# Squared norms of q and k: summed by products with a column of ones instead of a split and a row of ones

## The chip, the cores and the metric
One core of one Trainium2 chip. The metric is the device time of one execution in microseconds, the median of several runs. The engines are TensorE (PE: matmuls, with PEld for its weight loads), VectorE (DVE), ScalarE (ACT), GpSimd (POOL) and SyncE (SP), which mostly issues transfers.

## The reference
One step of a decoder layer with two groups of heads, for one prompt of 1024 tokens behind 16 meta tokens and for 8 running sequences of 4 tokens. All is float32. Of the inputs of the gated delta rule, q and k are normed by head:

```python
def l2norm(x):
    return x * lax.rsqrt(jnp.sum(x * x, axis=-1, keepdims=True) + EPS)
...
xn = rmsnorm(h, norm_mix)
z = xn @ w_in
qkv, new_qkv = causal_dwconv(z[..., O_QKV:O_G], buf_qkv, conv_qkv_w)
qkv = jax.nn.silu(qkv.astype(f32))
q = l2norm(qkv[..., :nq].reshape(bsz, t, GDN_HEADS, GDN_DK)) * (GDN_DK ** -0.5)
k = l2norm(qkv[..., nq:2 * nq].reshape(bsz, t, GDN_HEADS, GDN_DK))
```

There are 4 heads of 128 features for q and for k. Behind them stand the chunked delta rule, a norm with a gate, the output projection and a feed-forward part of 4096 hidden units.

## The kernel before
**Layout.** All 1072 tokens (32 of the samples, 16 meta, 1024 of the prompt) lie along the free axis, features along the partitions: `kf` and `qf` are 128 x 4 x 1072, a slice per head. Tokens come in nine tiles: tile 0 has the first 48 (`C0`), tiles 1 to 8 have 128 each. `GROUPS` are three runs of columns for matmuls: 304, 384 and 384 wide.

**Input projection.** `IN_TILES` lists 28 output tiles of 128 features: 4 of k, 4 of q, 4 of v, 4 of the gate, then 12 for the short convolution. Tile n and group g make unit u = 3n + g. Each unit is 24 dense matmuls (`dense_part`, L1341 to L1343: weights and activations are split in a high and a low fp32r part, three products for each of 8 slices). A loop over the 84 units is written out for each engine, and small work is hung on fixed units by hand. ScalarE takes k, q and v out of the banks, VectorE runs the causal convolution (`conv_tap`), ScalarE applies silu, and then makes the squares. GpSimd makes the low part of each weight tile (`w_low`), and SyncE's load of a later weight tile waits for that.

**The squared norms.** They have to be summed over the partitions and must stand with the tokens along the partitions in the end, as `dst[:, tile, head]`. For head j (0 to 3 are k, 4 to 7 are q): `square(j)` on ScalarE writes the float32 square and a copy rounded to fp32r; `square_low(j)` on VectorE (unit 6 + 3j) subtracts one from the other; `sum_squares(j)` on TensorE (unit 7 + 3j) moves the high and the low part through `pick`, a matrix of zeros with one column of ones that is placed so that each head and group has a row of its own among 12. After four heads `keep_rows` copies the 12 rows out of bank 7, `turn_squares` (units 17 and 29) turns them by nine transposes, and `keep_norms` adds EPS. ScalarE then takes roots, and `scale_norms_k` and `scale_norms_q` make the factors.

**Around it.** From unit 18 on, for each tile: `decay_rows` (L1463), `decay_diff` (L2109), the exp on ScalarE, from unit 19 on `products_kk` (L1476) and `keep_at` (L2117), and spills to DRAM by SyncE. `small_solve` (units 28, 29) and `solve` (units 30 to 38; L2137, L2139) on VectorE invert the triangular blocks by substitution; SyncE writes the result to `X_kept` and `Y_kept`. Tile 0's own steps stand at units 30 to 50: `sample_products` (L1600, units 36 and 37), `use_state0`, `next_state0` (L1625, L1626, unit 41), whose o goes through VectorE and ScalarE's squares (L1170). Then ScalarE loads At, X and Y for tile 1 (L1115 and on), and `level_p` (L1514) opens the first round at unit 42. `keep_last` (L1949) copies the last rows of the convolution, which `turn_last` (L1406) has turned.

Of the kernel before, what the change touches and what calls it, by code (L numbers as in the profile page):

```python
# [7 lines left out]
ALU = mybir.AluOpType  # L8
# [5 lines left out]
P = 128  # L14
# [79 lines left out]
def build(nc, x_prompt, x_sample, state_conv_a, state_conv_qkv, state_ssm, meta_tokens, norm_mix, w_in,  # L94
# [4 lines left out]
    with ctx:  # L99
# [14 lines left out]
        def place(name, shape, dt, offset):  # L114
            return nc.alloc_sbuf_tensor_at(name, shape, dt, offset=offset)
# [46 lines left out]
        abT = place("abT", [16, TOK], F32, RK + 4 * SLOT)  # L162

        sq = [place(f"squares{i}", [P, TOK], F32, RYA + i * SLOT) for i in range(2)]
        sq_h = [place(f"squares_high{i}", [P, TOK], F32R, RYA + (2 + i) * SLOT) for i in range(2)]
        sq_l = [place(f"squares_low{i}", [P, TOK], F32R, RYA + (4 + i) * SLOT) for i in range(2)]
        NROW = 3 * NH
        pick = place("pick", [P, 2 * NROW], F32R, RYA + 6 * SLOT)
        ssr = place("ss_rows", [NROW, 3 * P], F32, RYA + 7 * SLOT)

        cm = small("c_main", [P, 2 * P + 2 * C0 + 2 * NH])
        eye, upper = cm[:, 0:P], cm[:, P:2 * P]
# [128 lines left out]
        last_sent = [sem("last_sent0"), sem("last_sent1")]  # L301
        ya_high_s = sem("ya_high_s")
        ya_low_s = sem("ya_low_s")
        sq_full = sem("sq_full"); sq_high = sem("sq_high"); sq_low = sem("sq_low"); pick_set = sem("pick_set")
        ss_rows = sem("ss_rows"); ss_turned = sem("ss_turned"); ss_done = sem("ss_done")
        norms_mid = sem("norms_mid"); norms_root = sem("norms_root"); norms_done = sem("norms_done")
        s_levels = sem("s_levels"); s_ahead = sem("s_ahead"); s_states = sem("s_states")

# [449 lines left out]
        def _(pool):  # L758
# [98 lines left out]
                sh = SSs[h // 2][:, h % 2, :, :]  # L857
                pool.tensor_tensor(sh, sh, eg_seq[:, :, h:h + 1].to_broadcast([P, NSEQ, P]), ALU.mult).then_inc(ss_decayed, 1)

            def pick_column():  # L860
                pool.memset(pick[:, :].bitcast(F32), 0.0).then_inc(pick_set, 1)
                pool.wait_ge(pick_set, 1)
                pool.memset(pick[:, NROW:NROW + 1].bitcast(F32), 1.0).then_inc(pick_set, 1)

            for n in range(N_IN):
                kind, i, _ = IN_TILES[n]
                if kind in ("k", "q", "v"):
                    history(n)
                if n == 0:
                    pool.wait_ge(x_low, 3 * KT)  # L870
                    pick_column()
                if n == 1:
                    zero_pairs()
                if n == 2:
                    identities()
                if kind == "H":
                    history_a(i)
                if n + 1 < N_MIX:
                    split_low(n + 1)
                for u in range(3 * n, 3 * n + 3):  # L880
                    t, s = round_step(u)
                    if u == TILE0["k"]:
                        beside()
                    if u == TILE0["sample"][-1]:
                        decay_states(0)
                        decay_states(1)
                    if u == TILE0["use"]:
                        decay_states(2)
                        decay_states(3)
                    if u == TILE0["states"]:  # L890
                        power(0)
                    if s == 3 and t >= 2:
                        power(t - 1)
                    if u % 3 == 2 and has_last(n):
                        last_columns(n)
# [69 lines left out]
        def _(act):  # L965
# [67 lines left out]
            def square(j):  # L1033

                src = (kf if j < NH else qf)[:, j % NH, :]
                act.wait_ge(silu_done, j + 1)
                if j >= 2:
                    act.wait_ge(sq_low, j - 1)
                act.activation(sq[j % 2][:, :], src, ACT.Square).then_inc(sq_full, 1)
                act.wait_ge(sq_full, j + 1)  # L1040
                if j >= 2:
                    act.wait_ge(ss_done, j - 1)
                act.activation(sq_h[j % 2][:, :], sq[j % 2][:, :], ACT.Copy).then_inc(sq_high, 1)

            def norm_roots(i):
                n = sc[("nk", "rq_s")[i]]
# [287 lines left out]
        def _(pe):  # L1334
# [92 lines left out]
            def sum_squares(j):  # L1427

                if j == 0:
                    pe.wait_ge(pick_set, 2)  # L1430
                if j == NH:
                    pe.wait_ge(norms_mid, 1)
                pe.wait_ge(sq_low, j + 1)
                i = j % NH
                for m, g in enumerate((1, 0, 2)):
                    c0, w = GROUPS[g]
                    row = NH * g + i
                    for part in (sq_h, sq_l):
                        ins = pe.matmul(ps[7][0:NROW, 0:w], pick[:, NROW - row:2 * NROW - row], part[j % 2][:, c0:c0 + w],
                                        start=(i == 0 and m == 0 and part is sq_h),  # L1440
                                        stop=(i == NH - 1 and m == 2 and part is sq_l))
                ins.then_inc(ss_done, 1)

            def turn_squares(i):
                pe.wait_ge(ss_rows, i + 1)
                for t in range(NT):
                    o, c = tile_cols(t)
                    g = [t in x for x in GTILES].index(True)
                    o -= GROUPS[g][0]
                    ins = pe.transpose(ps[7][0:c, NROW * t:NROW * t + NROW], ssr[:, o:o + c], eye[0:NROW, 0:NROW])  # L1450
                ins.then_inc(ss_turned, 1)


            def decay_rows(t):

# [240 lines left out]
            for n in range(N_IN):  # L1696
                kind, i, _ = IN_TILES[n]
                for g in range(3):
                    u = 3 * n + g
                    if n:  # L1700
                        if g == 0:
                            pe.wait_ge(w_low, n + 1)
                        if u == 3:
                            pe.wait_ge(rows_kept, 3)
                        if u >= 4:
                            acc_free(pe, (u - 4) // 3, (u - 4) % 3)
                        dense_part(n, g, normed, range(KT))
                    if u == 5:
                        turn_ab()
                    if u == 8:  # L1710
                        sum_g()
                    if u % 3 == 1 and 7 <= u < 7 + 6 * NH:
                        sum_squares((u - 7) // 3)
                    if u in (17, 29):
                        turn_squares(0 if u == 17 else 1)
                    if ROWS_AT <= u < ROWS_AT + NT:
                        decay_rows(u - ROWS_AT)
                    if KK_AT <= u < KK_AT + NT:
                        products_kk(u - KK_AT)
                    if g == 2 and 1 <= n <= LAST_LAST:  # L1720
                        turn_last(n - 1, L_BANK)
                    tile0_step(u)
                    t, s = round_step(u)
                    if s:
                        round_part(t, s)
                    if u in TURN_H:
                        pe.wait_ge(vn_kept, min(t, NT))
                        turn_last(TURN_H[u], M_BANK)
# [156 lines left out]
        def _(dve):  # L1885
# [105 lines left out]

            nk, rk, c_, p_ = sc["nk"], sc["rk"], sc["c"], sc["p"]

            def square_low(j):
                dve.wait_ge(sq_high, j + 1)
                if j >= 2:
                    dve.wait_ge(ss_done, j - 1)
                dve.tensor_tensor(sq_l[j % 2][:, :], sq[j % 2][:, :], sq_h[j % 2][:, :].bitcast(F32),
                                  ALU.subtract).then_inc(sq_low, 1)

            def keep_rows(i):
                dve.wait_ge(ss_done, NH * (i + 1))
                dve.wait_ge(ss_turned, i)
                dve.tensor_copy(ssr[:, :], ps[7][0:NROW, 0:3 * P]).then_inc(ss_rows, 1)

            def keep_norms(i):

                dst = (nk, sc["rq_s"])[i]
                dve.wait_ge(ss_turned, i + 1)
                link(dve.memset(dst[:, 0, :], 1.0))  # L2010
                for g, ts in enumerate(GTILES):
                    turned = ps[7][:, 0:NROW * NT].rearrange("p (t r) -> p t r", r=NROW)
                    r0 = NH * g
                    if g == 0:
                        dve.tensor_scalar(dst[0:C0, 0, :], turned[0:C0, 0, r0:r0 + NH], EPS, None, ALU.add)
                        ts = ts[1:]
                    ins = dve.tensor_scalar(dst[:, ts[0]:ts[-1] + 1, :], turned[:, ts[0]:ts[-1] + 1, r0:r0 + NH],
                                            EPS, None, ALU.add)
                ins.then_inc(norms_mid, 1)

            def scale_norms_k():

# [331 lines left out]
            for n in range(N_IN):  # L2354
                kind, i, _ = IN_TILES[n]
                for g in range(3):
# [10 lines left out]
                        ab_second()  # L2367
                    if u == 9:
                        g_keep()
                    if u % 3 == 0 and 6 <= u < 6 + 6 * NH:  # L2370
                        square_low((u - 6) // 3)
                    if u in (16, 28):
                        keep_rows(0 if u == 16 else 1)
                    if u in (17, 29):
                        keep_norms(0 if u == 17 else 1)
                    if ROWS_AT <= u < ROWS_AT + NT:
# [194 lines left out]
```

## Time and profile before

| | us |
|---|---|
| median of 3 runs | 1363.97 (1362.43 to 1364.47) |
| the profiled execution's own time | 1363.06 |
| its span, first to last instruction | 1361.2 |
| TensorE matmul busy in it | 1329.1 |
| VectorE, ScalarE, GpSimd busy | 826.5, 413.6, 536.5 |

The rows below come from the profiled execution; its own time is 1.9 us above its span. A busy TensorE is not TensorE at its peak: matmuls are pipelined, so the time that one costs is the distance of its start from the next start, not the duration in its record. A product of plain float32 leaves two records, a transpose or an fp32r matmul one.

### The profile page before, as it was taken

The numbers are of one execution on the slowest core, as the hardware profiler recorded it, in microseconds if no ns is written. First come the engines' busy times: TensorE is split into PE (matmuls) and PEld (weight loads), VectorE is DVE, ScalarE is ACT, GpSimd is POOL, SyncE is SP. The second block draws the span as 40 slices with busy tenths as digits, with TensorE's granted clock in tenths as the row PEclk, the third lists the DMA queues.
The fourth block names the chain that finished last, engine by engine and source line by source line (L and its number), as shares of the span: only waits on it lengthen the run. The fifth ranks groups of instructions, "written<-read, shape, count | busy, mean of one in ns | idle before, by whom it ended". The sixth has DMA issues, their size and how long they took to land.

```text
span 1361.2 us, 22593 instructions
## 1 busy us (share of the span) xinstructions
PE 1329.1 (98%) x9089; PEld 1297.2 (95%) x9089; DVE 826.5 (61%) x1376; ACT 413.6 (30%) x812; POOL 536.5 (39%) x550
## 2 busy tenths in 40 slices
PE   6999999899999999999999999999999999999997
PEld 4899999799999999999999999999999999999997
DVE  4466689533644536555675666756666567566855
ACT  6566552111222212332032222222222223222312
POOL 2232123211112111211257557475674665746811
PEclk9999998999999999999999999999999999999999
DMA  6123553643332222321211212112012121111212
GB/s 189 38 67 101 145 156 101 153 135 83 83 88 63 78 71 75 91 80 37 57 31 47 63 32 63 47 47 63 32 47 63 32 64 37 57 47 34 77 43 117
DMA packets 161850, 99.88 MB, mean 73 GB/s; under 512 B 19639, under 2 KB 156371, under 8 KB 161746
## 3 DMA queue, kind: packets, MB, share of 16 engines
q1 hardware_dynamic: 137216, 85.31, 21.6%
q10 hardware_dynamic: 24530, 13.13, 3.6%
q8 instruction: 72, 1.18, 0.4%
q14 instruction: 32, 0.26, 0.1%
HBM read 77.62 MB, written 20.80 MB: 72 GB/s over the span
## 4 chain that ended last, share of the span: by engine, by line
PE 85%; DVE 7%; DMA 3%; ACT 2%; issue 1%; POOL 1%; SPq 1%; DVEq 0%; ACTq 0%; POOLq 0%
PE banks L1817 9%; PE banks L1819 9%; PE banks L1818 9%; PE banks L1341 8%; PE banks L1343 8%; PE banks L1342 8%; PE banks L1836 7%; PE banks L1837 7%; PE banks L1835 7%; DVE inverse L2139 2%; DVE outer L2137 2%; PE banks L1851 1%; PE banks L1514 1%; PE banks L1852 1%; PE banks L1853 1%
## 5 line engine op out<-in xcount | busy, mean ns | idle before, releaser
L1817 PE MATMUL banks<-hg_high,w_high 128*128 128x384 f32 (+1 forms) x768 | 249.5, 325 | 0.5 <-POOL w_low L906 0.5
L1819 PE MATMUL banks<-hg_high,w_low 128*128 128x384 f32 (+1 forms) x768 | 247.6, 322 | 0.0
L1818 PE MATMUL banks<-hg_low,w_high 128*128 128x384 f32 (+1 forms) x768 | 247.3, 322 | 0.0
L2474 DVE TENSOR_TENSOR hT<-hT,banks 128x528 f32<-128x528 f32 x280 | 189.5, 701 | 84.4 <-PE banks L1837 75.4
L1341 PE MATMUL banks<-xn_high,w_high 128*128 128x384 f32 (+1 forms) x672 | 228.0, 339 | 0.1
L1343 PE MATMUL banks<-xn_high,w_low 128*128 128x384 f32 (+1 forms) x672 | 219.8, 327 | 0.0
L1342 PE MATMUL banks<-xn_low,w_high 128*128 128x384 f32 (+1 forms) x672 | 219.8, 327 | 0.0
L774 POOL TENSOR_TENSOR w_low<-w_raw,w_high 128x1024 fp32r<-128x1024 f32 x37 | 90.5, 2447 | 265.4 <-ACT w_high L982 265.4
L1817 PEld LDWEIGHTS banks<-hg_high,w_high 128*128 128x128 f32 x768 | 144.2, 188 | 2.5 <-POOL w_low L906 2.3
L1818 PEld LDWEIGHTS banks<-hg_low,w_high 128*128 128x128 f32 x768 | 144.3, 188 | 0.1
L1819 PEld LDWEIGHTS banks<-hg_high,w_low 128*128 128x128 f32 x768 | 144.2, 188 | 0.0
L925 POOL TENSOR_TENSOR w_low<-w_pair,w_high 128x256 fp32r<-128x256 f32 x140 | 104.0, 761 | 67.0 <-ACT w_high L1296 67.0
L1341 PEld LDWEIGHTS banks<-xn_high,w_high 128*128 128x128 f32 x672 | 128.1, 191 | 2.0 <-DVE xn_low L1915 0.6
L906 POOL TENSOR_TENSOR w_low<-w_raw,w_high 128x1024 fp32r<-128x1024 f32 x31 | 78.7, 2537 | 126.8 <-ACT w_high L1278 126.8
L1342 PEld LDWEIGHTS banks<-xn_low,w_high 128*128 128x128 f32 x672 | 128.3, 191 | 0.0
L2453 DVE TENSOR_TENSOR u_row<-banks,h_squares 128x384 f32<-128x384 f32 (+1 forms) x96 | 50.1, 522 | 128.3 <-PE banks L1819 128.1
L1343 PEld LDWEIGHTS banks<-xn_high,w_low 128*128 128x128 f32 x672 | 127.7, 190 | 0.0
L1837 PE MATMUL banks<-op_high_T,w_low 128*128 128x264 f32 x448 | 127.7, 285 | 0.0
L1836 PE MATMUL banks<-op_low_T,w_high 128*128 128x264 f32 x448 | 127.7, 285 | 0.0
L1835 PE MATMUL banks<-op_high_T,w_high 128*128 128x264 f32 x448 | 127.1, 284 | 0.0
L1296 ACT ACTIVATE w_high<-w_pair 128x256 fp32r<-128x256 f32 x140 | 55.4, 415 | 177.9 <-PE banks L1819 84.6
L1837 PE MATMUL banks<-op_high_B,w_low 128*128 128x264 f32 x336 | 95.8, 285 | 0.0
(316 smaller groups left out, 2804.5 us busy)
## 6 DMA issues: line engine op xcount, KB each, us to landing
w_raw<-in_w_up SPq DMA_DIRECT2D x32, 512.0 KB, 4.1
w_pair<-in_w_down SPq DMA_DIRECT2D x32, 512.0 KB, 3.4
w_raw<-in_w_in SPq DMA_DIRECT2D x28, 512.0 KB, 4.4
w_raw<-in_w_out SPq DMA_DIRECT2D x8, 512.0 KB, 4.1
x_slice<-in_x_prompt SPq DMA_DIRECT2D x8, 512.0 KB, 4.1
out<-y_tok SPq DMA_DIRECT2D x8, 512.0 KB, 2.6
x_tok<-in_x_prompt SPq DMA_DIRECT2D x2, 1536.0 KB, 15.8
v_kept_rows<-v_feat SPq DMA_DIRECT2D x4, 536.0 KB, 3.2
```

The costliest lines, as they stand in the source:

```text
L774: pool.tensor_tensor(w_l[n % 2][:, :, :], w_raw[n % 2][:, :, :], w_h[n % 2][:, :, :].bitcast(F32), ALU.subtract).then_inc(w_low, 1)
L925: pool.tensor_tensor(set_of(w_l, b, s), set_source(n, PRODUCTS[x][0]), set_of(w_h, b, s).bitcast(F32), ALU.subtract).then_inc(w_low, 1)
L1341: pe.matmul(bank[:, 0:w], w_h[n % 2][:, k, :], hi[:, c0:c0 + w], start=(k == first), stop=False)
L1342: pe.matmul(bank[:, 0:w], w_h[n % 2][:, k, :], lo[:, c0:c0 + w], start=False, stop=False)
L1343: ins = pe.matmul(bank[:, 0:w], w_l[n % 2][:, k, :], hi[:, c0:c0 + w], start=False, stop=(k == last))
L1817: pe.matmul(bank[:, 0:w], w_h[half][:, k, :], hg_h[:, k, c0:c0 + w], start=(k == 0), stop=False)
L1818: pe.matmul(bank[:, 0:w], w_h[half][:, k, :], hg_l[:, k, c0:c0 + w], start=False, stop=False)
L1819: ins = pe.matmul(bank[:, 0:w], w_l[half][:, k, :], hg_h[:, k, c0:c0 + w], start=False, stop=(k == KT - 1))
L1835: pe.matmul(bank, high[:, j, :], op_h[name][:, j, cols], start=(j == 0), stop=False)
L1836: pe.matmul(bank, high[:, j, :], op_l[name][:, j, cols], start=False, stop=False)
L1837: ins = pe.matmul(bank, low[:, j, :], op_h[name][:, j, cols], start=False, stop=(j == FB // 2 - 1))
L2474: dve.tensor_tensor(hc, hc, both, ALU.add if sign > 0 else ALU.subtract).then_inc(acc_read_dve, 1)
```

## The change
The split and the turning fall away. `square(j)` makes only the float32 square. `sum_squares(j)` takes the square of each token tile as the stationary operand (128 x 128, or 128 x 48 for tile 0) and moves one column of ones, so that the sums come out with the tokens along the partitions, in column 8t + j of bank 7: nine plain float32 products for a head. `keep_norms` reads them from there.

```diff
-        sq_h = [place(f"squares_high{i}", [P, TOK], F32R, RYA + (2 + i) * SLOT) for i in range(2)]
-        sq_l = [place(f"squares_low{i}", [P, TOK], F32R, RYA + (4 + i) * SLOT) for i in range(2)]
-        NROW = 3 * NH
-        pick = place("pick", [P, 2 * NROW], F32R, RYA + 6 * SLOT)
-        ssr = place("ss_rows", [NROW, 3 * P], F32, RYA + 7 * SLOT)
...
-            def pick_column():
-                pool.memset(pick[:, :].bitcast(F32), 0.0).then_inc(pick_set, 1)
-                pool.wait_ge(pick_set, 1)
-                pool.memset(pick[:, NROW:NROW + 1].bitcast(F32), 1.0).then_inc(pick_set, 1)
...
                 if j >= 2:
-                    act.wait_ge(sq_low, j - 1)
+                    act.wait_ge(ss_done, j - 1)
                 act.activation(sq[j % 2][:, :], src, ACT.Square).then_inc(sq_full, 1)
-                act.wait_ge(sq_full, j + 1)
-                if j >= 2:
-                    act.wait_ge(ss_done, j - 1)
-                act.activation(sq_h[j % 2][:, :], sq[j % 2][:, :], ACT.Copy).then_inc(sq_high, 1)
...
             def sum_squares(j):
                 if j == 0:
-                    pe.wait_ge(pick_set, 2)
+                    pe.wait_ge(ab_kept, 2)
                 if j == NH:
                     pe.wait_ge(norms_mid, 1)
-                pe.wait_ge(sq_low, j + 1)
-                i = j % NH
-                for m, g in enumerate((1, 0, 2)):
-                    c0, w = GROUPS[g]
-                    row = NH * g + i
-                    for part in (sq_h, sq_l):
-                        ins = pe.matmul(ps[7][0:NROW, 0:w], pick[:, NROW - row:2 * NROW - row], part[j % 2][:, c0:c0 + w],
-                                        start=(i == 0 and m == 0 and part is sq_h),
-                                        stop=(i == NH - 1 and m == 2 and part is sq_l))
-                ins.then_inc(ss_done, 1)
-
-            def turn_squares(i):
-                pe.wait_ge(ss_rows, i + 1)
+                pe.wait_ge(sq_full, j + 1)
                 for t in range(NT):
                     o, c = tile_cols(t)
-                    g = [t in x for x in GTILES].index(True)
-                    o -= GROUPS[g][0]
-                    ins = pe.transpose(ps[7][0:c, NROW * t:NROW * t + NROW], ssr[:, o:o + c], eye[0:NROW, 0:NROW])
-                ins.then_inc(ss_turned, 1)
+                    ins = pe.matmul(ps[7][0:c, 2 * NH * t + j:2 * NH * t + j + 1], sq[j % 2][:, o:o + c], one[:, 0:1],
+                                    start=True, stop=True)
+                ins.then_inc(ss_done, 1)
...
-            def square_low(j):
-                dve.wait_ge(sq_high, j + 1)
-                if j >= 2:
-                    dve.wait_ge(ss_done, j - 1)
-                dve.tensor_tensor(sq_l[j % 2][:, :], sq[j % 2][:, :], sq_h[j % 2][:, :].bitcast(F32),
-                                  ALU.subtract).then_inc(sq_low, 1)
-
-            def keep_rows(i):
-                dve.wait_ge(ss_done, NH * (i + 1))
-                dve.wait_ge(ss_turned, i)
-                dve.tensor_copy(ssr[:, :], ps[7][0:NROW, 0:3 * P]).then_inc(ss_rows, 1)
...
             def keep_norms(i):
                 dst = (nk, sc["rq_s"])[i]
-                dve.wait_ge(ss_turned, i + 1)
+                sums = ps[7][:, 0:2 * NH * NT].rearrange("p (t j) -> p t j", j=2 * NH)[:, :, NH * i:NH * i + NH]
+                dve.wait_ge(ss_done, NH * (i + 1))
                 link(dve.memset(dst[:, 0, :], 1.0))
...
+                dve.tensor_scalar(dst[0:C0, 0, :], sums[0:C0, 0, :], EPS, None, ALU.add)
+                dve.tensor_scalar(dst[:, 1:NT, :], sums[:, 1:NT, :], EPS, None, ALU.add).then_inc(norms_mid, 1)
```

## Rows read from the trace of the kernel before

**Rows 1.** The page, busy us, share of the span and instructions.

```profile
PE 1329.1 (98%) x9089; PEld 1297.2 (95%) x9089; DVE 826.5 (61%) x1376; ACT 413.6 (30%) x812; POOL 536.5 (39%) x550
```

**Rows 2.** TensorE's waits: us in total, times, longest.

```profile
PE banks L1514 <- issue: 3.9, 1, 3.9
...
PE banks L1463 <- DVE decay L2109: 1.1, 1, 1.1
...
PE banks L1406 <- DVE last_out L1949: 0.5, 1, 0.5
```

**Rows 3.** Timelines of SyncE and ScalarE (start, us), DMA issues (KB, us to landing).

```profile
249.70 3.38 SPq L693 DMA_DIRECT2D Y_kept<-blocks  x1
...
Y_kept<-blocks SPq DMA_DIRECT2D x1, 512.0 KB, 8.2
...
256.44 0.19 ACT L1170 ACTIVATION_READ_ACCUMULATOR qs_scaled<-o_tok,rq_s 48x1 f32 x1
258.00 0.39 ACTq L1115 DMA_DIRECT2D At<-At_kept  x1
```

**Rows 4.** Timeline of VectorE, 177 to 248 us.

```profile
177.78 1.27 DVE L1998 TENSOR_TENSOR squares_low<-squares,squares_high 128x1072 fp32r<-128x1072 f32 x1 [2.66 <-ACT squares_high L1043]
178.97 1.12 DVE L2117 SCALAR_TENSOR_TENSOR At_spilled<-banks,p,decay 128x128 f32<-128x128 f32 x4
...
183.99 0.54 DVE L2004 COPY ss_rows<-banks 12x384 f32<-12x384 f32 x1
...
246.75 1.10 DVE L2142 COPY blocks<-inverse 128x1024 f32<-128x1024 f32 x1
```

**Rows 5.** Timeline of TensorE, one block of squares and one turning.

```profile
110.87 0.33 PE L1439 MATMUL banks<-squares_high,pick 128*12 128x384 f32 x1
...
111.84 0.33 PE L1341 MATMUL banks<-xn_high,w_high 128*128 128x384 f32 x1
...
115.85 0.34 PE L1343 MATMUL banks<-xn_high,w_low 128*128 128x384 f32 x1
116.12 0.69 PE L1450 MATMUL banks<-c_main,ss_rows 12*48 12x12 f32 x9
116.73 0.29 PE L1406 MATMUL banks<-c_main,last_in 128*27 128x128 f32 x1
```

**Rows 6.** Timeline of TensorE, the second half of the sample products.

```profile
227.15 3.64 PE L1600 MATMUL banks<-wq_sample,S_sample 128*128 128x8 f32 x32
230.64 0.42 PE L1341 MATMUL banks<-xn_high,w_high 128*128 128x384 f32 x1
230.90 0.34 PE L1342 MATMUL banks<-xn_low,w_high 128*128 128x384 f32 x1
```

**Rows 7.** Timeline of TensorE, `turn_ab`.

```profile
61.24 0.34 PE L1343 MATMUL banks<-xn_high,w_low 128*128 128x384 f32 x1
61.51 2.13 PE L1412 MATMUL banks<-c_main,abT 16*48 16x8 f32 x18
63.57 0.29 PE L1406 MATMUL banks<-c_main,last_in 128*27 128x128 f32 x1
```

**Rows 8.** Timeline of TensorE, decay rows and kk products at unit 19.

```profile
126.04 1.05 PE L1463 MATMUL banks<-c_main,g 128*128 128x128 f32 x8
127.03 0.56 PE L1476 MATMUL banks<-k_feat 128*48 128x48 f32 x8
```

**Rows 9.** Timeline of TensorE, the last kk products (unit 27).

```profile
174.85 1.05 PE L1476 MATMUL banks<-k_feat 128*128 128x128 f32 x8
```

**Rows 10.** Stretches: us, busy us of each engine, granted clock, DMA.

```profile
61.42:63.62 2.20, 2.20 (x21) 2.07 (x20) 0.00 (x0) 1.98 (x3) 0.98 (x5) 1.00 0.19 39
...
216.00:219.00 3.00, 2.84 (x27) 2.87 (x26) 2.90 (x4) 1.32 (x3) 2.48 (x3) 1.00 0.41 169
219.00:225.50 6.50, 6.50 (x24) 6.50 (x24) 6.12 (x13) 0.00 (x0) 0.51 (x1) 0.50 0.01 3
...
227.00:231.00 4.00, 4.00 (x36) 4.00 (x35) 3.79 (x9) 1.59 (x2) 0.14 (x1) 1.00 0.59 174
```

More of the change, by code:

```diff
@@ L303, in build @@
         ya_low_s = sem("ya_low_s")
-        sq_full = sem("sq_full"); sq_high = sem("sq_high"); sq_low = sem("sq_low"); pick_set = sem("pick_set")
-        ss_rows = sem("ss_rows"); ss_turned = sem("ss_turned"); ss_done = sem("ss_done")
+        sq_full = sem("sq_full")
+        ss_done = sem("ss_done")
         norms_mid = sem("norms_mid"); norms_root = sem("norms_root"); norms_done = sem("norms_done")
@@ L870, in _ @@
                     pool.wait_ge(x_low, 3 * KT)
-                    pick_column()
                 if n == 1:
@@ L1713, in _ @@
                         sum_squares((u - 7) // 3)
-                    if u in (17, 29):
-                        turn_squares(0 if u == 17 else 1)
                     if ROWS_AT <= u < ROWS_AT + NT:
@@ L1992, in _ @@
             nk, rk, c_, p_ = sc["nk"], sc["rk"], sc["c"], sc["p"]
-            def square_low(j):
-                dve.wait_ge(sq_high, j + 1)
-                if j >= 2:
-                    dve.wait_ge(ss_done, j - 1)
-                dve.tensor_tensor(sq_l[j % 2][:, :], sq[j % 2][:, :], sq_h[j % 2][:, :].bitcast(F32),
-                                  ALU.subtract).then_inc(sq_low, 1)
-            def keep_rows(i):
-                dve.wait_ge(ss_done, NH * (i + 1))
-                dve.wait_ge(ss_turned, i)
-                dve.tensor_copy(ssr[:, :], ps[7][0:NROW, 0:3 * P]).then_inc(ss_rows, 1)
             def keep_norms(i):
                 dst = (nk, sc["rq_s"])[i]
-                dve.wait_ge(ss_turned, i + 1)
+                sums = ps[7][:, 0:2 * NH * NT].rearrange("p (t j) -> p t j", j=2 * NH)[:, :, NH * i:NH * i + NH]
+                dve.wait_ge(ss_done, NH * (i + 1))
                 link(dve.memset(dst[:, 0, :], 1.0))
[L2011 to L2019, printed above, removed]
+                dve.tensor_scalar(dst[0:C0, 0, :], sums[0:C0, 0, :], EPS, None, ALU.add)
+                dve.tensor_scalar(dst[:, 1:NT, :], sums[:, 1:NT, :], EPS, None, ALU.add).then_inc(norms_mid, 1)
             def scale_norms_k():
@@ L2369, in _ @@
                         g_keep()
[L2370 to L2373, printed above, removed]
                     if u in (17, 29):
```

## Prediction
> **What bounds the kernel now.** I read the page first: TensorE is busy for 1329.1 of 1361.2 us [rows 1], so a microsecond of work put on it or taken from it is a microsecond of the end, unless a wait lies behind it that swallows it. So the next view is the list of TensorE's waits. The changed code runs between 61 and 190 us. Behind the first changed block only three waits are worth the name until the first round starts: 1.1 us for `decay_diff`, 0.5 us for `keep_last`, and the large one, 3.9 us of matmul idle before `level_p` (L1514) at 263 us [rows 2]. Everything on VectorE and ScalarE is of interest only where it feeds one of these.
>
> The third view is the chain of work, of which I took the pieces in order of time, and the timelines of VectorE, ScalarE and SyncE before 263 us. `level_p` waits for At. Its load is issued by ScalarE at 258.00 us. ScalarE has two things to get through before it: the squares of tile 0's o, whose last piece is at 256.44 us (they follow VectorE's o and that follows TensorE's `next_state0`, unit 41), and the landing of Y_kept, issued at 249.70 us and landed 8.2 us later, at 257.9 us [rows 3]. Y_kept landed last, and ScalarE had been free since 256.6 us: 1.3 us of slack on the branch that hangs on TensorE. Y_kept comes from the substitution on VectorE, which from 178.97 us to the copy at 246.75 us runs without a gap [rows 4].
>
> **What is removed from TensorE.** Eight blocks of six matmuls. One block stands from 110.87 to 111.84 us, so 0.97 us [rows 5]; the other seven have the same shapes: 8 x 0.97 = 7.8 us. Then twice nine turns: the matmul before them has its start at 115.85 us and passes the engine on 0.17 us later (the pitch of its neighbours), `turn_last` follows at 116.73 us: 0.70 us [rows 5], of which I leave 0.05 us for the change of operand that `turn_last` would then pay itself. 2 x 0.65 = 1.3 us. Together 9.1 us.
>
> **What is added to TensorE.** 72 float32 products, nine in a block, with a stationary tile of 128 x 128 (128 x 48 for tile 0) and one moving column. The trace has no product with one column, but two near ones. The sample products (L1600) have a 128 x 128 float32 stationary tile and 8 moving columns: 16 of them (32 records, so two for each product) take from 227.15 to 230.64 us, and the dense matmul behind them has a pitch of 0.26 instead of 0.17 us: 3.58 us, 0.224 us for one [rows 6]. `turn_ab` is nine products over the same nine tiles with 8 columns: from 61.41 us (61.24 and 0.17) to 63.57 us, 2.16 us [rows 7]. A product costs its loads of 128 columns here, not its columns, so one column costs as 8 do. For a block I take 2.1 us, between 9 x 0.224 = 2.02 and 2.16. 8 x 2.1 = 16.8 us. Bounds: from above four products with 128 columns, 126.04 to 127.03 us, 0.248 us for one, 2.23 us for a block [rows 8]; from below the nine turns, which have one record each, 0.70 us for nine [rows 5].
>
> Here a rule speaks against the change. The trace shows two records for each float32 product and 0.224 us. The Trainium skill (FP8 and Floating Point Precision, on how floating point is handled) says that true FP32 takes four passes through the array, and its page TensorE: Matmul & The Clock Gate (LDWEIGHTS) that a load costs its columns at 1.2 GHz, 107 ns for 128. If every pass had its load, a product would cost 0.43 us as an estimate from these pages, a block 3.9 us; the trace has half of it.
>
> **The sum on TensorE.** 16.8 - 9.1 = +7.7 us (with 2.02 and 2.16: +7.1 and +8.2; with 2.23: +8.7).
>
> **What the other engines get rid of.** VectorE loses eight subtractions of 1.27 us and two copies of 0.54 us [rows 4], ScalarE one pass over 128 x 1072 for each head, which stands in the same chain, GpSimd two small fills. Up to 178 us these lie beside TensorE's dense matmuls; the relief is worth nothing by itself, but it shortens the chain by which `decay_diff` is late. Nothing new is late by the added waits: TensorE now waits for the square itself (ready two instructions earlier than the low part), ScalarE's square of head j waits for a block of TensorE that ran two heads before.
>
> **What the waits swallow.** From block to block TensorE falls behind its old times by 1.13 us (2.1 - 0.97), while the decay chain beside it gets shorter. By the last decay rows (unit 26) it is some 6 us later, so I let the 1.1 us wait go. For `keep_last` TensorE waits for VectorE's program, and that moves less, see below: 0.5 us goes too [rows 2]. TensorE thus reaches unit 41 later by 7.7 - 1.1 - 0.5 = 6.1 us. ScalarE's squares end at 256.63 + 6.1 = 262.7 us, the load of At goes out there and not at 258.00 us: +4.7 us.
>
> The other branch: `keep_at(8)` at 178.97 us stands behind the subtraction of 1.27 us and the wait for ScalarE's high part; its product on TensorE is at 174.85 us for 0.9 us [rows 4, 9]. With seven blocks and one turning (7 x 1.13 - 0.65 - 1.1 = +6.2 us) it is ready at 181.9 us, so VectorE starts its gapless stretch 3.0 us later than now, and loses 0.6 us inside it (the copy at 183.99 us, 0.54 us [rows 4], and two small additions). Y_kept lands 2.4 us later, at 260.3 us: before 262.7 us, so it is not what ends last any more. Behind `level_p` the order of work and its waits are as before, and 4.7 us stay.
>
> The profiled execution took 1363.06 us with a span of 1361.2 us; the median of the runs is 1363.97 us. The sum gives a span of 1361.2 + 4.7 = 1365.9 us, 1367.8 us for the profiled execution, which is 0.9 us below the median, and 1363.97 + 4.7 = **1368.7 us** as the median (+0.3%).
>
> **The clock.** TensorE's granted clock fell to its half (1.2 instead of 2.4 GHz) once near such work: the first half of the sample products ran from 216.2 us, and from 219 to 225.5 us the clock is 0.50; in the second half, same size, it stayed at 1.00, as in `turn_ab` [rows 10]. A dip costs half of 6.5 us, 3.3 us. The new blocks have 2.1 us each, the size of `turn_ab`. But those of units 19, 22 and 25 are followed at once by decay rows and kk products, over 1 us of short float32 products [rows 8], together nearly as long as the sample half that lost the clock.
>
> **Rivals.**
> 1. *The waits are not swallowed* (chance 0.17). They move with TensorE, because what they wait for is released by TensorE itself (`decay_diff` by the decay rows, At through unit 41). Against it: `decay_diff` sheds a pass of ScalarE and the 1.27 us of VectorE for each head, and Y_kept, which ends last now, doesn't hang on unit 41. Price: the whole 7.7 us, 1371.6 us.
> 2. *A dip of the clock in units 19 to 25* (0.09): 4.7 + 3.3 = 8.0 us, 1372.0 us; with two, 1375 us.
> 3. *The dip at 219 us doesn't come back* (0.12), because the sample products start at another time. TensorE is then only 2.8 us late at unit 41, Y_kept at 260.3 us ends last, +2.4 us: 1366.4 us, within what counts as no change.
> 4. *Faster* (0.04): a product with one column costs less than one with 8, because it needs no second record. At the price of a turn, 0.078 us, a block costs 0.70 us, TensorE gains 9.1 - 5.6 = 3.5 us, and VectorE, which idled 2.66 us ahead of the subtraction at 177.78 us for its operand [rows 4], can start its stretch up to 3.9 us earlier, so that both branches of At come 3.5 us earlier: 1360.5 us. It decides below 9.1 / 72 = 0.126 us for a product.
> 5. *Four loads a product* (0.03). A block would be twice 2.1 us, TensorE 33.6 - 9.1 = +24.5 us, less the same 3.0 us of waits and slack: 1385.5 us. This is the case that the pages of the Trainium skill named above would give; the two records of L1600 speak against it.
>
> **How the numbers follow.** The likeliest case (0.55) has its own range by the bounds of a block, 2.02 to 2.23 us, and by half of the swallowed microsecond more or less: 1367.4 to 1370.5 us. 8 in 10 take in rival 3 below, and rival 1 and the single dip above: 1366.1 to 1372.4 us. The measurement tells 0.2%, 2.7 us, from no change. Slower by more than that: likeliest, 1, 2 and 5, 0.84. Within it: rival 3 and the low end, 0.12. Faster: 0.04.
>
> **What would show it.** In the profile after: blocks of 18 records on the line of `sum_squares`, 2.0 to 2.2 us from the dense matmul before to the one behind; TensorE's busy time up by some 7 us; no wait at `decay_rows`; `keep_at(8)` some 3 us later; the load of At at 262.7 us, behind the o squares and not behind Y_kept, and `level_p` at 268.2 us. It is wrong if a block takes under 1.2 or over 3 us, if the clock row shows a dip before 190 us, or if Y_kept still ends last.

## The result, and the profile after
The changed kernel takes 1371.49 us in the median of six runs (1370.08 to 1375.9), the kernel before 1363.97 us. The two medians differ by 7.5 us (0.55%), where 4.7 us were forecast; the ratio on record is 1.0064 (interval 1.0048 to 1.0079). In two later series of runs the same program stood at 1.0086 (1.0065 to 1.0108) and 1.0102 (1.0086 to 1.0117). A series (the expectations below say "call") is made on one chip, with the kernel before in it.

TensorE's busy time went from 1329.1 us [rows 1] to 1342.6 us in the page after, in a profiled execution of 1372.73 us, 9.7 us above that of before:

```profile
PE 1342.6 (98%) x9167; PEld 1313.7 (96%) x9167; DVE 821.7 (60%) x1362; ACT 405.8 (30%) x804; POOL 538.4 (39%) x548
```

The timeline of TensorE has the block as expected: a clean one (head 2) with 18 records, from 102.67 us (102.50 and the pitch, the distance from one start to the next, of 0.17) to 104.76 us, and a pitch of 0.26 us in place of 0.17 behind it, so 2.18 us against 0.97 us [rows 5]. And it has something that was not expected of a block that stands alone between dense matmuls. Behind head 0 the same dense matmuls have a pitch of 0.32 us in place of 0.17:

```profile
70.42 2.12 PE L1421 MATMUL banks<-one,squares 128*48 128x1 f32 x18
72.41 0.65 PE L1326 MATMUL banks<-xn_high,w_high 128*128 128x384 f32 x1
72.86 0.52 PE L1327 MATMUL banks<-xn_low,w_high 128*128 128x384 f32 x1
73.18 0.52 PE L1328 MATMUL banks<-xn_high,w_low 128*128 128x384 f32 x1
73.50 0.52 PE L1326 MATMUL banks<-xn_high,w_high 128*128 128x384 f32 x1
...
102.50 0.34 PE L1328 MATMUL banks<-xn_high,w_low 128*128 128x384 f32 x1
102.77 2.12 PE L1421 MATMUL banks<-one,squares 128*48 128x1 f32 x18
104.76 0.42 PE L1326 MATMUL banks<-xn_high,w_high 128*128 128x384 f32 x1
105.02 0.34 PE L1327 MATMUL banks<-xn_low,w_high 128*128 128x384 f32 x1
```

The table of stretches after shows what goes with it. Its third value from the right is the granted clock: 3.4 us at half the clock (1.2 in place of 2.4 GHz) behind four of the eight blocks, those of heads 0, 1, 3 and 5. The first trace of before has no such stretch in this part:

```profile
72.50:75.90 3.40, 3.40 (x12) 3.40 (x12) 0.00 (x0) 0.00 (x0) 0.00 (x0) 0.51 0.52 157
89.60:93.00 3.40, 3.40 (x13) 3.40 (x12) 0.00 (x0) 0.60 (x5) 0.00 (x0) 0.51 0.90 259
120.30:123.70 3.40, 3.40 (x12) 3.40 (x11) 0.00 (x0) 0.00 (x0) 0.00 (x0) 0.51 0.31 94
154.20:157.60 3.40, 3.40 (x18) 3.40 (x18) 1.13 (x4) 0.44 (x1) 0.00 (x0) 0.52 1.15 347
```

I call such a stretch a dip. One loses 3.4 / 2 = 1.7 us of TensorE's work. Added up, the clock lost between 60 and 240 us is 10.2 us here (four dips of 3.4 us and one of 6.8 us, halved) and 3.4 us in the trace of before (the one dip of [rows 10], which came again at 229 us).

Of TensorE's waits, the two small ones are gone and the large one has shrunk from 3.9 to 2.4 us [rows 2]; L1485 is `level_p`:

```profile
PE banks L1485 <- DMA At<-At_kept: 2.4, 1, 2.4
```

Both branches of At came late together, and Y_kept, not the squares, still ended last: it is issued at 258.48 us and lands 8.2 us later, at 266.68 us, and the load of At goes out at 266.74 us; before it was 258.00 us [rows 3]. ScalarE's squares of o began at 265.96 us and ran on past the load, so the load does not wait for the last of them. `keep_at(8)` waits for TensorE's product and starts at 187.45 us, not 178.97 us [rows 4]. The timelines of VectorE, SyncE and ScalarE after:

```profile
187.45 1.13 DVE L2068 SCALAR_TENSOR_TENSOR At_spilled<-banks,p,decay 128x128 f32<-128x128 f32 x4 [1.38 <-PE banks L1447]
...
258.48 3.38 SPq L688 DMA_DIRECT2D Y_kept<-blocks  x1
...
266.74 0.39 ACTq L1100 DMA_DIRECT2D At<-At_kept  x1
266.75 0.39 ACT L1155 ACTIVATE qs_scaled<-o_tok,rq_s 48x128 f32<-48x128 f32 x1
```

From the first product of `turn_ab` (61.51 us before [rows 7], 60.62 us after; the start-up varies) to the first of `level_p` it is 202.0 us before and 212.4 us after. Behind `level_p` nothing is added: from there to the end it is 1361.2 - 263.5 = 1097.7 us before and 1370.6 - 273.05 = 1097.5 us after.

### The profile page after: what moved, and what is told of

It is laid out like the page before. It is cut to its first block, busy times and chain, and to the rows that moved or that the text cites. A ratio compares the mean times of both kernels' runs of the same rounds, so it can differ in the third digit from the quotient of the medians.

```text
span 1370.6 us, 22712 instructions
## 1 busy us (share of the span) xinstructions
PE 1342.6 (98%) x9167; PEld 1313.7 (96%) x9167; DVE 821.7 (60%) x1362; ACT 405.8 (30%) x804; POOL 538.4 (39%) x548
## 4 chain that ended last, share of the span: by engine, by line
PE 93%; DVE 3%; DMA 2%; ACT 1%; issue 1%; SPq 0%; DVEq 0%; ACTq 0%
PE banks L1326 10%; PE banks L1328 10%; PE banks L1327 10%; PE banks L1786 9%; PE banks L1788 9%; PE banks L1787 9%; PE banks L1805 7%; PE banks L1806 7%; PE banks L1804 7%; PE banks L1421 1%; PE banks L1820 1%; PE banks L1821 1%; PE banks L1822 1%; PE banks L1485 1%; PE banks L1499 1%; DMA x_tok<-in_x_prompt 1%
## 5 line engine op out<-in xcount | busy, mean ns | idle before, releaser
L1326 PE MATMUL banks<-xn_high,w_high 128*128 128x384 f32 (+1 forms) x672 | 231.0, 344 | 0.1
```

Of the source, the lines that this page charges most:

```text
L1326: pe.matmul(bank[:, 0:w], w_h[n % 2][:, k, :], hi[:, c0:c0 + w], start=(k == first), stop=False)
```

## The experiments
The theory formed on this: **time = work of the products as far as the waits don't hide it, plus 1.7 us for each dip, and a narrow block of 2.2 us is long enough for dips.** "Narrow" means few moving columns. The rival, **plain work**: the products and their changes of operand cost all of it, and the dips only stand beside them. A second rival: only a single moving column lets the clock fall. Each ratio is against the kernel before in the same series; runs 1 to 4 are one series, 5 to 8 the next, 9 to 11 the last.

**1. Blocks cut in two.** The same 72 products, five behind unit 7 + 3j and four behind unit 8 + 3j.

```diff
-                for t in range(NT):
+                for t in range(*PARTS[part]):
...
+            PARTS = [(0, 5), (5, 9)]
```

> The changed kernel, with each head's nine products cut into five behind unit 7 + 3j and four behind unit 8 + 3j; the products and their number stay. Clock theory (a block of 2.1 us without a wide moving operand halves TensorE's granted clock for 3.4 us in about half of the cases, four times 1.7 us in the profile): pieces of 1.2 us cause no or hardly any dips, the granted clock stays 1.00 before 200 us, and the time is 1365 to 1367 us, 5 to 6 us below the changed kernel's 1371.5. Rival, plain work (the products and their change of operand cost all of it, the dips only stand beside them): two entries in place of one cost a little more, 1371 to 1373 us.

1368.29 us (1367.39 to 1371.67), ratio 1.0052 (1.0038 to 1.0065). No dip between 60 and 220 us. The clock did what the theory says; the time, 6.0 us above before (1362.26 us in that series), is not the 1 to 3 us above it that the theory asked for. The changed kernel did not run in this series, and the interval of this ratio overlaps its first one (1.0048 to 1.0079), so runs 9 and 10 have to settle what the cut gains.

**2. One by one between the dense matmuls** of unit 8 + 3j.

```diff
+                    if between:
+                        between(k)
...
-                        dense_part(n, g, normed, range(KT))
+                        product = sum_squares((u - 8) // 3) if u % 3 == 2 and 8 <= u < 8 + 6 * NH else None
+                        dense_part(n, g, normed, range(KT), between=product)
```

> The changed kernel, with each head's products put one by one between the dense matmuls of unit 8 + 3j, one behind each slice of three and the ninth at the end. Clock theory: no dip before 200 us at all, and the time falls to that of the two-part kernel, 1365 to 1367 us, plus or minus what nine changes between operands cost: if a product beside dense matmuls costs 0.22 us as in the block, the same time; if its first load hides behind the dense matmul ahead of it, 0.1 us less for each of 72, down to 1360 us; if each change of operand costs the 0.09 us seen behind a block, 1371 us with a clock of 1.00. Plain work: 1371 us or more.

1369.71 us, ratio 1.0051 (1.0039 to 1.0063). The table of stretches has no dip from 70 to 220 us (the one before 70 us is behind `turn_ab`):

```profile
60.00:70.00 10.00, 10.00 (x62) 9.71 (x61) 7.36 (x12) 7.70 (x12) 4.49 (x9) 0.83 0.09 19
70.00:220.00 150.00, 150.00 (x1020) 146.60 (x1020) 93.73 (x223) 77.88 (x126) 33.10 (x48) 1.00 0.43 118
```

The timeline of TensorE shows what a product costs there:

```profile
75.81 0.34 PE L1328 MATMUL banks<-xn_high,w_low 128*128 128x384 f32 x1
75.98 0.28 PE L1424 MATMUL banks<-one,squares 128*128 128x1 f32 x2
76.12 0.42 PE L1326 MATMUL banks<-xn_high,w_high 128*128 128x384 f32 x1
76.38 0.34 PE L1327 MATMUL banks<-xn_low,w_high 128*128 128x384 f32 x1
```

Without the product, the two dense matmuls behind that of 75.81 us would start at 75.98 and 76.15 us; the second one starts at 76.38 us, so the product costs 0.23 us, about as in the block (2.18 / 9 = 0.24 us). Nothing of it hides behind the dense matmuls. The run is 7.4 us above before with no dip behind a product, so the work is the larger part of the loss.

**3. Seven moving columns** in place of one.

```diff
-                    ins = pe.matmul(ps[7][0:c, 2 * NH * t + j:2 * NH * t + j + 1], sq[j % 2][:, o:o + c], one[:, 0:1],
+                    at = 7 * (2 * NH * t + j)
+                    ins = pe.matmul(ps[7][0:c, at:at + 7], sq[j % 2][:, o:o + c], one[:, 0:1].to_broadcast([P, 7]),
                                     start=True, stop=True)
```

> The changed kernel, with seven moving columns of ones in place of one (each sum is written seven times). Clock theory in its general form (any narrow block counts): the dips stay, a block takes 2.1 to 2.2 us, 1371 to 1372 us. Rival: only the single column lets the clock fall (turn_ab, with 8 columns and the same length, has none): the dips vanish, 1365 to 1367 us. Plain work: no change, 1371.5 us, dips or not.

1368.66 us (1367.74 to 1375.72), ratio 1.006 (1.004 to 1.008). In its profile one dip behind a block and one behind `turn_ab`, which moves eight columns. So a single column is not needed for a dip, and the second rival falls. Whether seven make dips rarer, one profile can't tell: the median is below the 1371 to 1372 us expected with dips, two of the six executions took 1374.56 and 1375.72 us at a mean clock of 0.985, against 0.991 to 0.993 in the others, and the ratio is within the interval of the changed kernel.

**4. The passes of ScalarE and VectorE put back**, read by nobody.

```diff
+                act.activation(sq_h[j % 2][:, :], sq[j % 2][:, :], ACT.Copy).then_inc(sq_high, 1)
...
+                dve.tensor_tensor(sq_l[j % 2][:, :], sq[j % 2][:, :], sq_h[j % 2][:, :].bitcast(F32),
+                                  ALU.subtract).then_inc(sq_low, 1)
```

> The changed kernel, with ScalarE's eight copies to fp32r and VectorE's eight subtractions put back, though nobody reads them. Clock theory, with the passes beside TensorE's work: 1371 to 1373 us, the load of At at the same place. Rival (the relief of the two engines shortens a wait and hides some of the products' cost): slower by 1 to 4 us, 1373 to 1375 us, with waits of TensorE for the decay or for At back.

1374.04 us, ratio 1.0087 (1.0073 to 1.01), five dips from 60 to 200 us. That is the ratio of the changed kernel in the next series (1.0086) and below that of the last (1.0102), with a mean clock of 0.986 to 0.987 (0.983 to 0.990 there); no wait for the decay came back. The table under 6 shows the same: with its five dips taken off it reaches the sample products when the changed kernel does. The relief of the two engines is worth nothing that these runs can tell, but since the changed kernel did not run in this series, a microsecond or two of the whole time stays open.

**5. The kernel before, again.** 

> The kernel before, once more, beside the others on one chip, to have its marks and its dips from a second execution. Both theories: a ratio of 1.000 within 0.1%, no dip of the granted clock between 60 and 200 us, one or two in the sample products, one behind the wait for At; the first product of turn_ab between 59.5 and 61.5 us, since the start-up varies.

1363.76 us, ratio 1.0001 (0.9993 to 1.001). The expectation of no dip from 60 to 200 us missed: this execution has two there, one of them behind `turn_ab` (0.83 from 60 to 70 us in the table of stretches), the other behind a wait of 2.2 us for the decay:

```profile
60.00:70.00 10.00, 10.00 (x61) 9.96 (x61) 6.77 (x10) 9.12 (x15) 4.37 (x9) 0.83 0.04 9
...
170.00:176.00 6.00, 5.59 (x31) 5.49 (x32) 5.06 (x17) 4.00 (x6) 0.51 (x4) 0.72 0.50 148
```

`turn_ab`, the same block in the same program, has a dip in this execution and none in the first.

**6. The changed kernel, again.** 

> The changed kernel, once more, on the same chip. Clock theory: dips of 1.7 us each behind some of the eight blocks again, not behind the same ones, since they depend on where the block happens to fall; the executions differ by such steps; from turn_ab to the first sample product 159.9 us (two parts, no dip) plus 1.7 us for each dip; median 0.6 to 0.7% above before. Rival, plain work: the same distance with and without dips.

1374.0 us (1369.94 to 1380.18), ratio 1.0086. The results list a mean granted clock for each execution: 0.990 for 1369.94 us, 0.989 for 1373.53 and 1373.8, 0.987 for 1374.2, 0.984 for 1379.31, 0.983 for 1380.18. 0.007 of some 1370 us is 9.6 us, and the times differ by 10.2 us: as far as three decimals tell, the lost clock is paid in full. Its profile, of the fastest of them, has one dip behind `turn_ab` and three behind blocks, at 104, 172 and 193 us (heads 2, 6 and 7); in the first profile they were behind heads 0, 1, 3 and 5.

What the expectation set against plain work is the distance from the first product of `turn_ab` to the first of the sample products, read from the timeline of TensorE in each profile:

| profile | dips in between | distance, us |
|---|---|---|
| before; before, again | 0; 2 | 154.65; 157.90 |
| two parts (run 1; run 10) | 0; 1 | 159.95; 161.50 |
| between the dense matmuls (2) | 1 | 161.66 |
| seven columns (3) | 2 | 163.36 |
| changed kernel, first profile; again (6) | 4; 4 | 166.59; 166.53 |
| passes put back (4) | 5 | 168.05 |
| changed kernel, third time (9) | 6 | 169.62 |
| three parts (11) | 1, and a wait of 1.7 us | 163.21 |

From the two parts with no dip to the whole blocks with six it grows by 9.7 us, 1.6 us for each; the three parts come under 9 to 11. Without dips the change costs 159.95 - 154.65 = 5.3 us here, in two parts; with 1.6 us for each dip taken off, the whole blocks and the single products come to the same within 0.3 us. Plain work would have the same distance with and without dips, so this tells against it most directly.

**7. The kernel before without the low part** (the sums are those of squares rounded to fp32r).

```diff
-                act.activation(sq[j % 2][:, :], src, ACT.Square).then_inc(sq_full, 1)
-                act.wait_ge(sq_full, j + 1)
...
-                act.activation(sq_h[j % 2][:, :], sq[j % 2][:, :], ACT.Copy).then_inc(sq_high, 1)
+                act.activation(sq_h[j % 2][:, :], src, ACT.Square).then_inc(sq_high, 1)
...
-                    for part in (sq_h, sq_l):
```

> The kernel before without the low part: ScalarE writes the square rounded to fp32r, VectorE subtracts nothing, TensorE moves three runs of columns for a head instead of six; the sums are those of the rounded squares. TensorE loses 8 x 0.49 = 3.9 us of wide matmuls and no block is narrow. Clock theory: no dip, time 3 to 4 us below before as far as the wait for At lets it through, 1359 to 1362 us. Rival (Y_kept, not TensorE, sets the load of At, and it hangs on VectorE): VectorE's stretch starts earlier too, by the subtraction and its wait of 2.7 us, so the gain passes; if the stretch hung on the decay chain instead, no gain, 1362 to 1363 us.

1357.91 us (1357.18 to 1358.12), ratio 0.9958 (0.9945 to 0.997): 5.7 us faster, more than the 3.9 us of its matmuls. Y_kept goes out at 241.28 us and not at 249.70 us [rows 3]: VectorE's branch gained more than TensorE's (reckoned from `turn_ab`, `keep_at(8)` starts 8.0 us earlier and the first sample product 6.3 us), and At is loaded at 250.97 us. TensorE still waits 4.4 us there.

**8. The changed kernel with rounded squares** (the sums are those of squares rounded to fp32r): the square is written as fp32r, and two columns of ones in fp32r move.

```diff
-        sq = [place(f"squares{i}", [P, TOK], F32, RYA + i * SLOT) for i in range(2)]
+        sq = [place(f"squares{i}", [P, TOK], F32R, RYA + i * SLOT) for i in range(2)]
+        ones_r = place("ones_rounded", [P, 2], F32R, RYA + 6 * SLOT)
...
-                    ins = pe.matmul(ps[7][0:c, 2 * NH * t + j:2 * NH * t + j + 1], sq[j % 2][:, o:o + c], one[:, 0:1],
+                    ins = pe.matmul(ps[7][0:c, at:at + 2], sq[j % 2][:, o:o + c], ones_r[:, 0:2],
```

> The changed kernel with the square rounded to fp32r by ScalarE as the stationary operand and two columns of ones in fp32r moving; the sums are those of the rounded squares. It keeps the form of the block and halves its records: one load for each product, 0.08 to 0.11 us, a block of 0.8 to 1.1 us as in the turns of before. Clock theory: blocks so short cause no dip; TensorE has 8 x 1.0 = 8 us instead of 9.1 us: 1360 to 1363 us, at or 1 us below before. Plain work: the same by another road (half of 17.4 us is gone): 1362 to 1363 us; it is told apart from the clock theory by the clock alone, here.

1357.39 us (1355.26 to 1359.11), ratio 0.9956 (0.9943 to 0.9968). The timeline has one record for a product, a block of 70.93 - 70.01 = 0.92 us and 0.09 us of longer pitch behind it:

```profile
70.01 1.06 PE L1426 MATMUL banks<-ones_rounded,squares 128*48 128x2 f32 x9
70.93 0.42 PE L1328 MATMUL banks<-xn_high,w_high 128*128 128x384 f32 x1
71.19 0.34 PE L1329 MATMUL banks<-xn_low,w_high 128*128 128x384 f32 x1
```

The table of stretches has a clock of 1.00 up to 200 us:

```profile
60.00:200.00 140.00, 140.00 (x952) 138.04 (x951) 92.07 (x217) 83.04 (x131) 36.06 (x57) 1.00 0.43 119
```

It was forecast at 1360 to 1363 us: the work is as forecast, and the rest goes with VectorE's earlier start (`keep_at(8)` 5.1 us earlier, reckoned from `turn_ab`), as in 7. This version and 7 beat both kernels, with the sums rounded; the runs don't tell which of the two is faster.

**9 to 11. Whole blocks, two parts and three parts in one series.** The third kernel has three products behind each of the units 7, 8 and 9 + 3j (`PARTS = [(0, 3), (3, 6), (6, 9)]`).

> The changed kernel, a third time, so that the two cuts of its blocks stand beside it on one chip. Time theory now: before + 6 us for the work of the products, as far as waits don't hide it, + about 1.6 us for each dip beyond those of before; with three to five dips 1370 to 1374 us, and within its executions the slower ones have the lower mean clock (0.983 for 1380 us, 0.990 for 1370 us in the execution list of the second call). Rival: the mean clock doesn't order them.

> The blocks of nine cut into five and four, again. Time theory: 6 us above before, mean clock as before (0.992 to 0.994), so 2 to 5 us below the whole blocks in the same call. Rival, plain work: no difference from the whole blocks.

> The blocks of nine cut into three times three, behind units 7 + 3j, 8 + 3j and 9 + 3j. Time theory: the dips were already gone with two parts, so that a third entry only adds its change of operand, 8 x 0.1 to 0.2 us: 6 to 8 us above before, clock as before. Rival (the dips get rarer with every cut): below the two parts by 1 to 2 us.

| | median | ratio | clock lost, 60 to 218 us, in the profile |
|---|---|---|---|
| before, same series | 1362.67 | | |
| whole blocks | 1374.93 (1373.82 to 1379.4) | 1.0102 (1.0086 to 1.0117) | 10.2 us, six dips, one of them behind `turn_ab` |
| two parts | 1369.69 (1367.78 to 1374.09) | 1.0056 (1.0044 to 1.0069) | 1.7 us, one dip, behind `turn_ab` |
| three parts | 1372.97 (1371.88 to 1375.32) | 1.0076 (1.0064 to 1.0088) | none; one dip at 219.28 us |

The tables of stretches of the whole blocks and of the two parts:

```profile
90.00:100.00 10.00, 10.00 (x58) 9.93 (x58) 1.78 (x4) 4.91 (x10) 1.60 (x4) 0.83 0.43 107
...
145.00:165.00 20.00, 20.00 (x134) 19.74 (x133) 11.33 (x29) 10.28 (x15) 2.48 (x2) 0.91 0.50 140
165.00:185.00 20.00, 20.00 (x133) 19.74 (x132) 11.97 (x31) 9.58 (x14) 2.83 (x5) 0.91 0.51 143
185.00:205.00 20.00, 20.00 (x130) 19.66 (x129) 16.80 (x54) 10.63 (x16) 4.88 (x7) 0.91 0.39 104
```

```profile
60.00:70.00 10.00, 10.00 (x61) 9.71 (x61) 7.40 (x12) 7.75 (x12) 4.49 (x9) 0.83 0.11 26
70.00:200.00 130.00, 130.00 (x898) 127.03 (x897) 74.75 (x182) 69.42 (x111) 30.26 (x43) 1.00 0.38 104
```

One cut, with the same 72 products, takes 5.2 us off the median, and the dips behind blocks with it: plain work falls. In run 9 too the slower executions have the lower mean clock (0.989 for 1373.82 us, 0.984 for 1378.97 and 1379.4 us).

A second cut has no dips left to take and costs 3.3 us. The changes of operand are not the reason: at 203.99 us, at a product of `turn_last` behind the last block, the three parts are 143.3 us behind `turn_ab`, and the two parts of run 1 are 143.5 us behind it at the same product (203.30 us). What comes then stands in the profile of the three parts: `keep_norms` for q on VectorE waits 4.7 us for the last three products, in the stretch that ran without a gap before (0.8 us in the two parts), and TensorE waits 1.7 us for `keep_last`, where the two parts don't wait. Behind that wait stands a dip. The lines are of VectorE's timeline, TensorE's waits and the stretches:

```profile
194.77 0.06 DVE L1973 MEMSET rq_s<- 128x4 f32 x1 [4.72 <-PE banks L1423]
...
PE banks L1391 <- DVE last_out L1923: 1.7, 1, 1.7
...
218.00:224.00 6.00, 6.00 (x34) 5.95 (x35) 5.69 (x13) 3.06 (x5) 0.99 (x3) 0.72 0.59 184
```

The wait and the dip together make the 163.21 - 159.95 = 3.3 us by which the three parts reach the sample products later than the two parts of run 1. This is one profile, and no run put the last products back to test it.

## Why the prediction was off
**The step that failed is the one on the clock.** It says that the new blocks have the size of `turn_ab`, where the clock stayed at 1.00, sees a danger only in units 19, 22 and 25, where short products follow, and gives it a chance of 0.09; the sum itself has nothing for it. Three of the four dips of the first profile are behind blocks that stand between dense matmuls (heads 0, 1 and 3). Over the three profiles of the changed kernel it is 5 of 9 blocks in units 19, 22 and 25 and 7 of 15 of the others, so what follows a block made no difference that can be seen. `turn_ab` itself has a dip in 6 of the 13 profiles, among them that of the kernel before, again: one trace of one execution was read as a property of the block. The runs give for it 5.2 us between whole blocks and two parts in one series, and three to five dips of 1.7 us behind the blocks in each of the three profiles. Each was half of what the prediction priced, 3.3 us, which is the dip of 6.8 us in [rows 10].

**The work of the products** was right in kind and a little small: 2.18 us for a block, not 2.1 us, 8 x 0.08 = 0.6 us more. By the sample products the change without dips is 5.3 us late, in the profile of run 1, where 6.1 us were forecast. In whole times the two parts stand 6.0 and 7.0 us above before, against the 4.7 us forecast; some of their executions have dips too, as the profile of run 10 shows, and how the rest divides is open.

**The waits** for the decay and for `keep_last` went as forecast, and that at `level_p` shrank [rows 2]. So rival 1, whose 1371.6 us is nearly the measured time, is not what happened: the waits did swallow their part, and the dips put as much back. Its number was right by accident.

**At's two branches.** Without dips, VectorE's branch moved as worked out: in the first run of the two parts `keep_at(8)` starts 2.8 us later than before, reckoned from `turn_ab` (180.10 - 59.83 against 178.97 - 61.51 us), where 3.0 us were forecast. But the 0.6 us that the stretch was to lose did not show: it ran to 249.08 us, 1.2 us longer than before, 0.8 us of it a wait of `keep_norms` for the products of the second part. Y_kept took 9.2 us to land, not 8.2, and still ended last there, with At loaded at 261.30 us; TensorE waited 5.1 us for it. The other branch was read wrong: the prediction lets the load of At wait for the last of the squares of o (256.44 us before, which gives 1.3 us of slack). In run 6, where Y_kept lands at 264.75 us, before the squares, the load goes out 0.1 us behind the start of the first of them:

```profile
265.59 0.40 ACT L1155 ACTIVATE qs_scaled<-o_tok,rq_s 48x128 f32<-48x128 f32 x1 [3.27 <-DVE o_tok L2187]
265.69 0.39 ACTq L1100 DMA_DIRECT2D At<-At_kept  x1
```

Before, that first square starts at 254.97 us, so the slack was 2.9 us. "Behind the o squares and not behind Y_kept" was wrong in the first profile as well, where Y_kept lands at 266.68 us and the first square starts at 265.96 us.

**The relief** of VectorE and ScalarE was put at nothing for this kernel, and run 4 shows nothing. In runs 7 and 8, where TensorE does not fall behind, the time fell by more than TensorE's own gain: 5.7 us against 3.9, and 6.2 against 9.1 - 8 x 1.01 = 1.0 us. In both profiles the waits for the decay and for `keep_last`, 1.6 us together [rows 2], are gone and At is loaded earlier (250.97 and 252.06 us). That the rest is the relief is argued from this, not shown by a run of its own.

**Four loads a product** (rival 5): the blocks have two records a product and 0.24 us, so twice the 2.1 us of a block is not what is paid, in any of the runs. With the square rounded, a product leaves one record and takes 0.11 us. Whether there are four passes, as the Trainium skill has it (FP8 and Floating Point Precision, TensorE Precision Notes), no run here shows. If there are, they don't each cost the 107 ns of a load that its page TensorE: Matmul & The Clock Gate (LDWEIGHTS) gives for 128 columns: four would be an estimate of 0.43 us, and the traces have 0.24 us.

## What to carry to other kernels
A product with a large stationary tile and one moving column cost as much here as one with seven or eight (0.24 us in float32 with 128 stationary columns), so 72 of them cost more than 48 wide fp32r matmuls and 18 transposes. And runs of such products of 2.1 us between dense matmuls cost clock as well, in half of the cases; cut into pieces of 1.3 us or less they did not, and lengths between were not tried. Look where the last piece goes, since another engine may be waiting for it, as in the three parts. Don't take the absence of a dip from one trace as a promise, but look at the mean clock of all executions. Where an operand may be rounded, ask for that first: here it was worth 6 us against before, and 16.6 us against the plain float32 form in the same series.

## What the runs showed of the hardware
Each dip has the same size, 3.4 us at half the clock (or twice that, as at 219 us in [rows 10]), apart from the last one, which the end of the execution cuts off, and stands behind different blocks in each execution. In the 13 profiles, up to 200 us, dips followed blocks of nine narrow float32 products, 2.1 us long (`turn_ab` in 6 of 13, the blocks of the changed kernel 12 times in 24, one of eight with seven columns, five of eight with the passes put back), and one wait of 2.2 us. None followed a piece of five, four or three products, or a single one, even where such a piece ran straight into decay rows and kk products, 2.9 us of short products in all (units 22 and 25 of the two parts). From 200 to 240 us they followed the sample products, and once the wait of 1.7 us in the three parts. Within six executions of one program the time followed the mean granted clock from 0.990 (1369.94 us) to 0.983 (1380.18 us).

The Trainium skill (TensorE: Matmul & The Clock Gate, HAM oscillation) describes a clock that falls again and again in a kernel with few rows, and puts it down to TensorE waiting for data. The dip behind the wait of 2.2 us for the decay in run 5 agrees in kind; behind the blocks TensorE was not waiting, and the records stand back to back.
